# Queries and keys of the mLSTM made transposed, two heads a group

## What is computed

```python
proj = h @ w_in                                   # h = rmsnorm(x), 256 x 1024
qk = silu(causal_depthwise_conv(proj[..., :1024], conv_w, conv_b))   # 4 taps along the positions
q, k = qk[..., :512], qk[..., 512:]               # 4 heads x 128 each
v, o_pre = proj[..., 1024:2048], proj[..., 2048:3072]
i_pre, log_f = gates + b_i, log_sigmoid(gates + b_f)                 # 8 columns of proj
ht = mlstm_chunkwise(q, k, v, i_pre, log_f)       # decayed scores, values, running maximum
out = (sigmoid(o_pre) * rmsnorm(ht)) @ w_out
```

## Time and profile before

| | |
|---|---|
| median of 3 runs | 1145.24 us (1144.76 to 1146.21) |
| profiled execution | 1145.26 us, span 1143.5 us |
| TensorE (PE) | 1137.5 us busy, 99% |
| VectorE (DVE) | 757.6 us busy, 66% |
| ScalarE (ACT) | 629.3 us busy, 55% |
| GpSimd (POOL) | 64.3 us busy, 6% |
| granted TensorE clock | 1.000 |
| DMA | 203.49 MB, 178 GB/s mean |

### The profile page before, as it was taken

How to read it: one execution, slowest core, us unless ns; L and a number is a source line. 1 busy time by engine, 2 the same in 40 slices (tenths; PEclk the granted TensorE clock), 3 DMA queues, 4 the chain that set the end, 5 groups by cost and what they waited for, 6 DMA issues and landing times.

```text
span 1143.5 us, 15945 instructions
## 1 busy us (share of the span) xinstructions
PE 1137.5 (99%) x5744; PEld 957.7 (84%) x5744; DVE 757.6 (66%) x1033; ACT 629.3 (55%) x966; POOL 64.3 (6%) x75
## 2 busy tenths in 40 slices
PE   9999999999999999999999999999999999999998
PEld 6788888888888888888898887888888888888887
DVE  5977756656685666655679879665755667566565
ACT  6687554445568555444556455656654455454344
POOL 3001100000000100000030042000000000000000
PEclk9999999999999999999999999999999999999999
DMA  9644566565554566666557555444656556666642
GB/s 306 192 135 129 178 191 197 185 188 196 161 165 157 165 190 196 187 193 190 182 177 225 176 174 159 141 118 128 182 191 195 182 176 186 192 192 192 193 156 102
DMA packets 99542, 203.49 MB, mean 178 GB/s; under 512 B 7902, under 2 KB 19830, under 8 KB 99489
## 3 DMA queue, kind: packets, MB, share of 16 engines
q1 hardware_dynamic: 98144, 199.68, 56.4%
q0 software_dynamic: 1184, 3.04, 0.9%
q10 hardware_dynamic: 160, 0.07, 0.0%
HBM read 201.70 MB, written 1.06 MB: 177 GB/s over the span
## 4 chain that ended last, share of the span: by engine, by line
PE 98%; DVE 1%; ACT 0%; DMA 0%; issue 0%; SPq 0%
PE pair L755 17%; PE pair L757 17%; PE pair L756 17%; PE pair L878 8%; PE turn_ps L878 8%; PE score L756 4%; PE score L757 4%; PE score L755 4%; PE pair L876 3%; PE turn_ps L876 3%; PE turn_ps L786 3%; PE pair L1192 3%; PE pair L1190 1%; PE turn_ps L881 0%; PE pair L881 0%; DMA x<-in_x 0%
## 5 line engine op out<-in xcount | busy, mean ns | idle before, releaser
L1864 DVE TENSOR_TENSOR w_lo<-raw,w_hi 128x1024 fp32r<-128x1024 f32 (+2 forms) x380 | 455.4, 1223 | 179.5 <-ACT w_hi L1385 178.4
L1385 ACT ACTIVATE w_hi<-raw 128x1024 fp32r<-128x1024 f32 (+2 forms) x380 | 390.2, 1049 | 230.8 <-DMA raw<-in_mlp_w 88.0
L755 PE MATMUL pair<-w_hi,a_both 128*128 128x512 f32 (+3 forms) x464 | 184.7, 398 | 0.0
L757 PE MATMUL pair<-w_hi,a_both 128*128 128x512 f32 (+3 forms) x464 | 178.4, 385 | 0.0
L756 PE MATMUL pair<-w_lo,a_both 128*128 128x512 f32 (+3 forms) x464 | 177.9, 383 | 0.0
L878 PE MATMUL pair<-a_both,w_hi 128*128 128x512 f32 x384 | 141.9, 394 | 0.0
L878 PE MATMUL turn_ps<-a_both,w_hi 128*128 128x512 f32 x384 | 141.9, 394 | 0.0
L757 PEld LDWEIGHTS pair<-w_hi,a_both 128*128 128x128 f32 x464 | 87.1, 188 | 17.5
L755 PEld LDWEIGHTS pair<-w_hi,a_both 128*128 128x128 f32 x464 | 87.2, 188 | 16.2 <-ACT work L1430 0.3
L756 PEld LDWEIGHTS pair<-w_lo,a_both 128*128 128x128 f32 x464 | 87.4, 188 | 15.3 <-issue 0.2
L876 PE MATMUL pair<-a_both,w_lo 128*128 128x256 f32 x336 | 93.8, 279 | 0.0
(11 more groups left out here) (423 smaller groups left out, 1845.3 us busy)
## 6 DMA issues: line engine op xcount, KB each, us to landing
raw<-in_mlp_w SPq DMA_DIRECT2D x128, 512.0 KB, 4.3
raw<-in_w_in SPq DMA_DIRECT2D x64, 512.0 KB, 3.7
raw<-in_w_up SPq DMA_DIRECT2D x32, 512.0 KB, 3.8
raw<-in_w_down SPq DMA_DIRECT2D x32, 512.0 KB, 3.4
raw<-in_attn_w_in SPq DMA_DIRECT2D x24, 512.0 KB, 6.4
raw<-in_mlstm_w_in SPq DMA_DIRECT2D x24, 512.0 KB, 3.7
raw<-in_w_br SPq DMA_DIRECT2D x16, 512.0 KB, 3.4
raw<-in_attn_w_out SPq DMA_DIRECT2D x8, 512.0 KB, 3.3
```

The lines of the kernel that those rows point to most:

```text
L755: pe.matmul(o, hi, whi, start=start, stop=False)
L757: return pe.matmul(o, lo, whi, start=False, stop=stop)
L1385: act.activation(w_hi[:, k % RING, 0:n], raw[:, k % RING, 0:n], ACT.Copy).then_inc(hi_ready, 1)
L1864: dve.tensor_tensor(w_lo[:, k % RING, 0:n], raw[:, k % RING, 0:n], w_hi[:, k % RING, 0:n], ALU.subtract).then_inc(lo_ready, 1)
```

## The change

Queries and keys become four groups of 256 columns (mq0, mq1, mk0, mk1; two heads each, two units of four chunks), made by the transposed form, whose function moves up and is named `turned_dense`. The order of the units becomes mq0, mq1 (first halves), mq0, mq1 (second halves), gate, mk0, mk1, mv0 and so on. For each of the four groups ScalarE copies the second half of the bank (copy_part), VectorE adds it to the first half (sum_parts) and multiplies by the factor of the positions (scale_rows). The factor is spread by GpSimd over 128 columns, transposed by TensorE (row_turn) and copied by ScalarE (row_copy). The convolution reads the result from SBUF. conv_turn is gone.

```diff
-    group("gate", ml, 3 * D, 2 * ML_H, "x2", DC, 1, 0, per=8, last=0)
-    group("mq", ml, 0, HALF, "x2", DC, 2, 0, last=DC - 2)
-    chunks("gate", 0, DC)
-    chunks("mq", DC - 2, DC)
-    for name, col in (("mk", HALF), ("mv0", D), ...
+    for n in range(2):
+        group(f"mq{n}", ml, n * S, S, "x2", DC, 1, 1, per=4, last=DC // 2)
+    for n in range(2):
+        chunks(f"mq{n}", DC // 2, DC)
+    group("gate", ml, 3 * D, 2 * ML_H, "x2", DC, 1, 0, per=8)
+    for n in range(2):
+        group(f"mk{n}", ml, HALF + n * S, S, "x2", DC, 1, 1, per=4)
+    for name, col in (("mv0", D), ...
...
 # TensorE
+            def turned_dense(name, slots=None, part=slice(None)):
+                ps = group_ps(name) if part.start else open_pair(name)
+                def unit(u):
+                    k, c0, n = u
+                    pe.wait_ge(lo_ready, k + 1)
+                    for j in range(n):
+                        c = c0 + j
+                        wait_source(groups[name]["source"], c)
+                        for b in range(2):
+                            cols = slice((2 * j + b) * P, (2 * j + b + 1) * P)
+                            if c:
+                                pe.matmul(ps[:, b, S:], w_lo[:, k % RING, cols], a_hi[:, c, :], ...)
+                            last = pe.matmul(ps[:, b, :], w_hi[:, k % RING, cols], a_both[:, c, :, :], ...)
...
+            def row_turn():
+                pe.wait_ge(row_spread, 1)
+                transposed("rowT", [row_cols[:, tt, :] for tt in range(TT)])
...
-            dense("mq", {0: lambda: (x_turn(2, 4), x_turn(2, 6))}, slice(0, 3))
+            turned_dense("mq0", {0: lambda: (x_turn(2, 4), x_turn(2, 6))}, one)
+            turned_dense("mq1", None, one)
+            turned_dense("mq0", None, two)
+            turned_dense("mq1", None, two)
             gate_dense()
-            dense("mq", {3: gate_turn}, slice(3, 4))
-            dense("mk", {1: cumulate, 2: lambda: (rows_turn(0), conv_turn(0)), 3: lambda: (spread(0), conv_turn(1))})
-            dense("mv0", {1: lambda: rows_turn(1), 2: lambda: (spread(1), conv_turn(2)), 3: lambda: conv_turn(3)})
+            turned_dense("mk0", {0: lambda: (gate_turn(), row_turn())})
+            turned_dense("mk1", {0: cumulate, 1: lambda: rows_turn(0)})
+            dense("mv0", {0: lambda: spread(0), 2: lambda: rows_turn(1), 3: lambda: spread(1)})
...
 # ScalarE
+            def copy_part(name):
+                wait_group(act, name)
+                act.wait_ge(group_dve, groups[name]["dve_end"] - 1)
+                act.activation(qk_part[:, :, :], group_ps(name)[:, :, S:], ACT.Copy).then_inc(group_act, 1)
...
+            dense("mq0", {0: lambda: (split_turn("x2.4"), split_turn("x2.6"))}, one, AHEAD // 2)
+            dense("mq1", {0: lambda: x_squares(2)}, one, AHEAD_0)
+            dense("mq0", None, two, AHEAD_0)
+            copy_part("mq0")
+            dense("mq1", None, two)
+            copy_part("mq1")
             dense("gate")
...
-            dense("mk", {0: gate_log, 2: lambda: (rows_copy(0), convolve(0)), 3: lambda: convolve(1)})
-            empty("mk", [ml_qk[:, 1, tt, :] for tt in range(TT)], scales=row_norm(2))
-            dense("mv0", {1: lambda: rows_copy(1), 2: lambda: convolve(2),
-                          3: lambda: (convolve(3), weights(), silu(0), silu(1))})
+            dense("mk0", {0: row_copy, 1: gate_log})
+            copy_part("mk0")
+            dense("mk1", {0: lambda: convolve(0), 1: lambda: (rows_copy(0), convolve(1))})
+            copy_part("mk1")
+            dense("mv0", {1: lambda: convolve(2), 2: lambda: (rows_copy(1), convolve(3)), 3: lambda: (silus(), weights())})
+            act.wait_ge(rstd_ready, 3)
             empty("mv0", half_v(0), scales=row_norm(2))
-            dense("mv1", {0: lambda: silu(2), 1: lambda: silu(3)})
+            dense("mv1")
...
 # VectorE
-                        src = turn_bank(name)[:, j * S:(j + 1) * S - shift]
+                        src = ml_qk[:, b, j, 0:S - shift]
...
+            def sum_parts(b):
+                dve.wait_ge(group_act, groups[name]["act_end"])
+                dve.tensor_tensor(ml_qk[:, b, :, :], group_ps(name)[:, :, 0:S], qk_part[:, :, :], ALU.add)\
+                    .then_inc(group_dve, 1)
+            def scale_rows(b):
+                dve.wait_ge(turn_act, turn["rowT"]["act_end"])
+                dve.wait_ge(group_dve, groups[name]["dve_end"])
+                dve.tensor_tensor(ml_qk[:, b, :, :], ml_qk[:, b, :, :], spread_to(row_t[:, :], 1, [2, S]), ALU.mult)\
+                    .then_inc(ml_keyed, 1)
...
-            dense("mk", {0: ml_log_forget, 1: ml_cumulated, 2: lambda: convolve(0),
-                         3: lambda: (ml_maxima(), convolve(1))})
-            dense("mv0", {2: lambda: (ml_arguments(), convolve(2)), 3: lambda: convolve(3)})
+            dense("mq0", None, two, AHEAD_0)
+            sum_parts(0)
+            dense("mq1", None, two)
+            sum_parts(1)
+            dense("gate")
+            dense("mk0", {0: ml_gates, 1: lambda: (ml_log_forget(), scale_rows(0))})
+            sum_parts(2)
+            dense("mk1", {0: lambda: (ml_cumulated(), convolve(0), scale_rows(1)), 1: lambda: convolve(1)})
+            sum_parts(3)
+            dense("mv0", {0: lambda: (scale_rows(2), ml_maxima(), scale_rows(3)), 1: lambda: convolve(2),
+                          2: lambda: convolve(3), 3: ml_arguments})
...
 # GpSimd, behind x_factor(2)
+            pool.wait_ge(rstd_ready, 3)
+            pool.tensor_copy(row_cols[:, :, :], rstd[:, 2, :].unsqueeze(2).to_broadcast([P, TT, P])).then_inc(row_spread, 1)
```

## The result

The changed kernel takes 1147.3 us (median of 15 runs, 1146.9 to 1148.3) against 1145.2 of before (15 runs, 1144.8 to 1146.9): ratio 1.0019, 95% interval 1.0013 to 1.0026. It is slower by 2.1 us. The profiled execution took 1147.14 us, its span is 1145.3, which is 1.8 more than before.

What follows compares the result with a forecast made beforehand. The prediction took TensorE, busy 99% of the span, to bound the kernel. From 1145.26 us, -0.79 (its own work) + 2.25 and 1.45 (two stalls) - 0.1 (old wait) gave 1148.1 us, own range 1147.2 to 1149.3.

Steps and rivals of the forecast that it cites:

- TensorE's own work: Turned units +0.60 us, 16 conv transposes gone -1.57, row_turn's two transposes +0.18: -0.79 us if nothing waited.
- First wait: TensorE's rows_turn(1) waits for VectorE to end ml_maxima, now behind more queued work: 2.25 us where 0.1 stood.
- Taps at 2.34 a set: VectorE's convolution taps keep their time, 2.34 us a set, though they now read SBUF, not PSUM.
- cheaper taps: Rival: VectorE's 24 convolution taps get shorter from SBUF, 0.055 us each at midway; 1146.8 us, chance 0.15.
- Second wait: TensorE's dense("mo0") waits for ScalarE to empty mv0's banks, after ml_arguments and weights(): 1.45 us.
- The gate waits: Rival: gate_dense on TensorE waits 1 us for late loads or sum_parts(0), forecast at 0; 1149.0 us, chance 0.10.
- GpSimd's spread costs 0: GpSimd's spread of the factor has over 7 us of cover before it is wanted, so it costs 0.
- Sum: All terms against the profiled 1145.26 us: -0.79 + 2.25 + 1.45 - 0.1 = +2.8, giving 1148.1 us.
- The clock falls: Rival: after the stall one TensorE unit runs at 1.2 GHz, 5.4 us and not 2.7; 1150.8 us, chance 0.04.
- my signs of being right: rows_turn(1) waiting over 2 us, mo0 1 to 2, turned units at 2.80, mq0 to mv1 longer by 2.8 us.
- those of being wrong: Taps clearly under 0.39, ml_maxima before 337, mo0 without wait, TensorE idle ahead of the gate, clock below 1 after 336.
- No stalls: Rival: neither TensorE wait comes and only TensorE's own sum counts; 1144.4 us, chance 0.10.

Runs made afterwards that it cites:

- e8: Changed kernel with scale_rows on GpSimd, ml_arguments ahead of convolve(3), sum 3 behind ml_maxima, weights() ahead of the last two silus: 1144.00 us, ratio 0.9988.
- e1: Changed kernel with two extra, unread VectorE sums of 128x512 just ahead of ml_maxima: 1149.33 us, ratio 1.0037 to the kernel before.
- e2: Changed kernel with two extra, unread VectorE sums of 128x512 behind ml_arguments: 1147.83 us, ratio 1.0021 to the kernel before.
- e3: Changed kernel without the four scale_rows, so queries and keys lack the norm's factor: 1145.51 us, ratio 1.0001 to the kernel before.
- e6: Changed kernel with the four scale_rows on GpSimd, orders otherwise the same: 1145.75 us, ratio 1.0002 to the kernel before.
- e5: Changed kernel with three more copies of 128x512 on ScalarE between the silus and weights(): 1148.03 us, ratio 1.0026 to the kernel before.
- e10: The changed kernel itself, measured again beside the version with the filled wait: 1147.64 us, ratio 1.0019 to the kernel before.
- e9: Changed kernel with ten unread matmuls of zeros on TensorE in its wait ahead of rows_turn(1): 1147.32 us, ratio 1.0018 to the kernel before.
- e7: Changed kernel reordered: VectorE ml_maxima ahead of convolve(1), ml_arguments ahead of convolve(2); ScalarE rows_copy(1) and two silus ahead of convolve(2), weights() ahead of the last two: 1144.39 us.
- e4: Changed kernel with ml_maxima moved back ahead of convolve(1) on VectorE, all else the same: 1148.67 us, ratio 1.0032 to the kernel before.

## Why the prediction was right, and where it was not

The forecast was 1148.1 (own range 1147.2 to 1149.3), the time is 1147.3, just inside. The two waits came where they were forecast; the size of the second was wrong by more than a microsecond, and the clock wasn't expected to fall. Its steps, each against its row:

- **TensorE's own work, -0.79.** Measured -0.87. A turned unit is 302.62 - 299.82 = 2.80, as forecast. e8 shows the sum without the two stalls, -0.96.
- **First wait, 2.25 us in place of 0.1.** Measured 2.54. VectorE's chain was to run from 324.5 to 338.4 and ran from 324.66 to 338.74; cumulate started at 323.90 and not 323.7. The cause is shown from both sides, by e1 and e2 (more ahead, more wait; more behind, no more) and by e3 and e6 (less ahead, less wait).
- **Taps at 2.34 a set, from SBUF as from PSUM.** Measured 327.72 - 325.36 = 2.36. The median tap took 472 ns from PSUM and takes 478 from SBUF. So the source brought nothing, and "cheaper taps" was no cause of anything here. The rule of the Trainium skill (VectorE: DVE Perf Modes, The TRN2 errata) that SBUF operands cost 58 cycles of fixed time and PSUM ones 120 is not what these rows show: 6 ns in the other direction.
- **Second wait, 1.45 us.** This is the term that was mis-sized: it measured 0.32. I took weights() whole, 4.88 us, from ml_arguments on, because in the earlier trace rows it runs in one piece. But its first 1.28 us, the table load, needs no operand, and ScalarE was idle ahead of it. From ml_arguments' end only 3.5 us of exponentials and 1.25 of emptying follow. The earlier trace rows could have told it: ACT_TABLE_LOAD is a row of its own, and my own text had ScalarE waiting there. e5 put the load back on the path and got the 1.2 us.
- **The gate waits: 0 with no margin.** Nearly right: its first matmul starts 0.17 us late (311.59, the last one ahead of it, and 0.23, to 311.99), and this is in the -0.87. The profile puts it down to issue, but the rows below say that it is the forecast one, for sum_parts(0): the gate's first weight load starts 0.07 us behind the end of that sum (311.89, forecast 311.8), and 0.06 to 0.08 behind it in the traces of all ten experiments too; before, it started at 308.64, 0.23 ahead of its matmul. So there was no margin, as I wrote, and the wait cost under 0.2.

```profile
311.21 0.68 DVE L2255 TENSOR_TENSOR ml_qk<-pair,qk_part 128x512 f32<-128x512 f32 x1
...
311.96 0.19 PEld L1164 LDWEIGHTS pair<-a_both,w_hi 128*128 128x128 f32 x1 [0.30 <-issue]
```

- **GpSimd's spread costs 0.** Right; it took 1.31 us, twice VectorE's row that I had as the lower bound, with 7 us of cover.
- **Sum.** -0.87 + 2.45 + 0.32 = +1.90, against +2.8. The sum was 0.9 too high: 1.1 at the second wait, for the table load, and 0.1 at TensorE's own work, less 0.3 at the first wait.
- **"The clock falls", chance 0.04, price 2.7 (1150.8).** It fell in 6 of 11 runs of e10, and in the changed kernel's 15 runs the upper group has 7. So the chance was far too small and the price too large. It costs about 1.0 (1147.0 to 1148.0): in e2's profile the lower level held for eight of the unit's twelve matmuls, and the wait at mo0 gave 0.3 back. I rested on the earlier trace rows, where TensorE idles 2.17 of 8 us at 1.00. But that is a sum of gaps: TensorE's longest wait in the whole kernel before is 1.2 us, the one for the zeros at the start. No row of before had a single gap of 2.4 us, and I should have said so and given the case more. The Trainium skill (TensorE: Matmul & The Clock Gate, HAM oscillation) has idle gaps that put the array to half rate; e2's rows agree, and e9, with the gap filled, has no such execution. With this second effect the forecast lies among the changed kernel's longer runs, but by two errors that offset each other, not by its own sum; against the runs at full clock (1147.0) it is 1.1 too high. And those runs lie mostly below my own range of 1147.2 and more: that the median falls into it is in part luck, the upper group's.
- **The chances and the signs.** I set 2.3 us as the least that tells a change and gave "slower" 0.63 and "same" 0.34. The difference is 2.1: by that limit it is "same", though the interval lies clear of 1. Of my signs of being right, the first wait and the turned units came true; the second wait (1 to 2 us) and the longer stretch (2.8) did not. Of those of being wrong, TensorE's idling ahead of the gate came true with 0.17 us, and the clock below 1 behind 336 in about half of the executions; the profile of e2 shows it there.
- **No stalls, 1144.4.** It was not the case, but it is close to the times of the versions whose orders are repaired: 1144.4 (e7) and 1144.0 (e8).

## What to carry to other kernels

A helper at 66% busy sets the time if one result in its queue is awaited: write out its queue from the last forced start to that result, add what a change puts ahead of it, and compare with the awaiting engine's own schedule to the tenth of a microsecond. Before adding up a block of work behind a wait, strike from it what needs no operand of that wait; and before repairing one engine's order, follow the next two hand-overs, since the wait goes to where the next engine's order is still the old one. An idle time of 2.4 us on TensorE cost 1.0 us more than itself in about half of the executions here, so look at the granted clock right behind such a wait.

## What the runs showed of the hardware that I had not expected

- **ScalarE's table load ran ahead of the wait of the activation behind it**: load 347.04 to 348.32, operand ready at 348.69, exponential at 348.72. Where the operand is there already, load and exponential are 1.30 us apart (347.86 to 349.16 in e5). The Trainium skill (ScalarE: Activation LUTs, What ACT_TABLE_LOAD costs) gives 1283 ns for the load, with which the rows agree, and some 1380 ns of draining beside it, of which they show nothing.
- **Idle time and TensorE's clock.** Behind 2.4 us of idle time the clock was at 1.2 GHz for a while in about half of the executions. Behind 3.2 us (e4) it was so in the profiled one, from 1.3 us behind the end of the wait on, and behind 3.8 us (e1) for nearly a whole unit; behind 1.4 and 1.5 (e3, e6) it was at 2.4 GHz in the profiled ones.
- **GpSimd and VectorE seem to slow each other in some places.** A product of 128x512 takes GpSimd 1.3 us in one place and 2.2 in another. In e8 it ran beside two w_lo of VectorE, which took 3.45 us and not 2.36. In e6 one of 128x8 on VectorE took 0.64 and not 0.17: it ended with GpSimd's (325.31 and 325.29), which is why I take it to be delayed by it, though no experiment tested that. And it isn't always so: beside e6's third product (332.27, 2.21 us) VectorE's w_lo took its usual 1.22. The rows of e6, GpSimd first, then VectorE:

```profile
323.09 2.20 POOL L2692 TENSOR_TENSOR ml_qk<-ml_qk,row_t 128x512 f32<-128x512 f32 x1 [0.77 <-DVE ml_qk L2255]
```

```profile
324.67 0.64 DVE L2202 TENSOR_TENSOR ml_g<-gate_in,ml_g 128x8 f32<-128x8 f32 x1
```

The delayed operation is one of ml_cumulated's, ahead of ml_maxima, so e6 pays for it in its wait. (In e8 the same one took 0.85, where the order leaves room.) In e8 the 1.1 us fall behind the maxima, where nobody waits.
